# HGRN's score tasks laid at chosen places of the RWKV steps in the scans of a hybrid token mixer

## The chip, the cores and the metric

The kernel runs on one core of a Trainium2 chip. The metric is the device time of one execution in microseconds. The kernel before was timed three times: 5044.99, 5073.87 and 5080.72 us, median 5073.87 us.

## The reference

One layer over 2048 latent tokens and 256 context tokens, all float32: a normed and modulated input is projected, goes through two kinds of scans in both directions, is read out, and a mixture of experts follows. Only the scans matter here.

```python
# HGRN, 4 heads of 128, for each direction, in chunks
bc = cumsum(logf)                                    # within a chunk
o  = (q * exp(bc)) @ s + (causal scores of q, k with decay exp(bc_t - bc_s)) @ v
s  = exp(bc_last) * s + (k * exp(bc_last - bc)).T @ v

# RWKV-7, 8 heads of 64, for each direction, token by token
sa = s @ kk_t
s  = s * w_t - outer(sa, kk_t * a_t) + outer(v_t, k_t)
y_t = s @ r_t
```

The context's final states start the scans of the latent tokens, so each direction of each scan is one chain over 2304 tokens.

## The kernel before, in words

The stages follow one another: modulation, RWKV's projection, HGRN's projection with RWKV's preparation, masks, **scans**, read-out, experts, combination. The diff touches the scans (`scans`, which calls `both_scans` on each engine).

HGRN works in steps of 128 tokens (`HG_STEPS` = 18), RWKV in steps of 64 (`RW_STEPS` = 36), both directions d = 0 and 1 side by side. One turn of `both_scans` is one HGRN step beside two RWKV steps; two turns stand ahead of the loop, and the loop's body holds two.

An RWKV step (`RwkvScan`) does two things. It computes the inverse of a unit triangular matrix of its 64 tokens for every head, by levels: gram products (L1432), a mask on VectorE (L1570), the masks of each level on GpSimd (L1554), a first inverse (L1579), a turn (L1441), and then for the levels 1 to 5 a **cross** product on TensorE (L1453), its copy X on ScalarE (L1514), a **grow** product on TensorE (L1461, L1464) and the **update** of the inverse on VectorE (L1585, at level 5 L1587). Each of these needs the one before it. Beside it runs the chain of the step before: rhs (L1380), solve (L1391), out (L1401), state (L1415), with ScalarE's copies of rhs, u and y (L1492, L1498, L1504) and VectorE's state (L1593). `RW_ORDER` lists the stages of a step; each is done for direction 0 and then for direction 1.

An HGRN step (`HgrnScan`) has 16 tasks t: seven levels and the diagonal, for two directions (t odd is direction 1). At its start ScalarE takes logarithms (L362) and, once VectorE has summed them (L497), a block of exponentials (L370 to L373), with a table load ahead of each; GpSimd multiplies them onto k and q (L399, L401). For each task from 2 on VectorE takes a difference of sums (L474), ScalarE its exponentials (L379, L380), GpSimd the scaled q and k (L411, L412), TensorE the **score** product (L429), VectorE the placing into the scores (L482, L486, L490). Behind scores 3 and 4 TensorE transposes k (L439), which ScalarE copies (L385). At the end come both outputs and states (L450 to L459), copied by ScalarE (L390) and added by VectorE (L509).

What sets the order on each engine is a stream of times. Every generator yields a nominal time ahead of each piece of its work, and `side_by_side` always takes the stream with the smallest time, at build time; on the chip each engine executes its list strictly as written, waiting on semaphores. A turn is 1.0 long; RWKV's steps lie at 0 to 0.5 and 0.5 to 1. The same generators are used for all engines, so each engine's list follows from the same times. The loads (`sync`) are issued by SyncE in a fixed order and aren't part of these streams: RWKV's loads of a step wait until the state of two steps before is done.

```python
def hg_time(t):
    return 0.10 + 0.048 * t
def rw_time(name, d, later=0.0):
    return (2 * RW_ORDER.index(name) + d + 0.5 + later) / (2 * len(RW_ORDER))
```

HGRN's own times: logarithms at 0, sums at 0.02, the block of exponentials at 0.045, score t at `hg_time(t)`, its difference 0.12 before, its exponentials 0.08 before, GpSimd's products 0.04 before, the placing 0.03 after, outputs at 0.90 and 0.95.

Of the kernel before, what the change touches and what calls it, by code (L numbers as in the profile page):

```python
# [92 lines left out]
def peel(eng, count, body):  # L93

    body(0)
    if count > 1:
        with eng.Fori(1, count) as g:
            body(g)
# [201 lines left out]
HG_LOG, HG_SUM, HG_ENDS, HG_OUT = 0.0, 0.02, 0.045, 0.90  # L300


def hg_time(t):

    return 0.10 + 0.048 * t
# [927 lines left out]
def side_by_side(*streams):  # L1233

    live = [[next(x), k, x] for k, x in enumerate(streams)]
    while live:
        first = min(live, key=lambda e: e[0:2])
        first[0] = next(first[2], None)
        if first[0] is None:
            live.remove(first)  # L1240


def shifted(stream, start, scale):

    for time in stream:
        yield start + scale * time
# [62 lines left out]
RW_ORDER = ("gram0 rhs gram1 turn cross1 solve grow1 cross2 out grow2 cross3 grow3 state cross4 grow4 cross5 grow5").split()  # L1309
# [300 lines left out]
                f(d)  # L1610


def both_scans(eng, h, r):

    def turn(g):
        for u in range(2):
            k = 2 * g + u
            two = itertools.chain(shifted(r(eng, 2 * k, 0), 0.0, 0.5), shifted(r(eng, 2 * k + 1, 1), 0.5, 0.5))
            side_by_side(two, shifted(h(eng, k, u), 0.25, 1.0))
    peel(eng, HG_STEPS // 2, turn)  # L1620


def scans(nc, A, S, K):
    with ExitStack() as ctx:
        h, r = HgrnScan(nc, Mem(nc, ctx, "hg"), S, K), RwkvScan(nc, Mem(nc, ctx, "rw"), S, K)
        with nc.Block() as block:
# [10 lines left out]
            @block.gpsimd  # L1637
            def _(pool):
                both_scans(pool, h.pool, r.pool)
                r.store(pool, RW_STEPS)  # L1640
                for d in range(2):
                    pool.wait_ge(r.s[d]["y_stored"], 16 * RW_STEPS)

            @block.scalar
            def _(act):
                both_scans(act, h.act, r.act)
                drain(r.act(act, RW_STEPS, 0, True))
                for d in range(2):
                    act.wait_ge(h.s[f"stored{d}"], 16 * HG_STEPS)

            @block.tensor
            def _(pe):
                both_scans(pe, h.pe, r.pe)
                drain(r.pe(pe, RW_STEPS, 0, True))
# [1085 lines left out]
```

## Time and profile before

| | |
|---|---|
| median of three runs | 5073.87 us (5044.99 to 5080.72) |
| the profiled execution | 5056.55 us, span 5055.0 us |
| TensorE busy | 4322.2 us, 86% of the span |
| VectorE, ScalarE, GpSimd busy | 2222.9, 1249.3 and 1571.8 us |
| mean granted TensorE clock | 0.932 |
| the scans | about 1475 to 3120 us of the span |

A program prints the profile from one execution recorded by the hardware. PE is TensorE, DVE VectorE, ACT ScalarE, POOL GpSimd, PEld TensorE's weight loads. A matmul in float32 leaves two records, so the 16 products of 8 heads and two directions are 32 records. In a timeline row stand the start in us, the length of a merged group of instructions, engine, line, operation, what it writes and reads, the shape and the number of records; in brackets the idle time before it and what ended it. In a row of waits stand who waited, for whom, the us in total, the times and the longest. In a row of stretches each engine has its busy us and its number of instructions; behind them come the granted clock (1.00 is full), the share of DMA and GB/s. "issue" is time for which the profile shows nothing that was waited for.

### The profile page before, as it was taken

The numbers are of one execution on the slowest core, as the hardware profiler recorded it, in microseconds if no ns is written. First come the engines' busy times: TensorE is split into PE (matmuls) and PEld (weight loads), VectorE is DVE, ScalarE is ACT, GpSimd is POOL, SyncE is SP. The second block draws the span as 40 slices with busy tenths as digits, with TensorE's granted clock in tenths as the row PEclk, the third lists the DMA queues.
The fourth block names the chain that finished last, engine by engine and source line by source line (L and its number), as shares of the span: only waits on it lengthen the run. The fifth ranks groups of instructions, "written<-read, shape, count | busy, mean of one in ns | idle before, by whom it ended". The sixth has DMA issues, their size and how long they took to land. (4 is left out here: it accounts for less than half of the span.)

```text
span 5055.0 us, 123964 instructions
## 1 busy us (share of the span) xinstructions
PE 4322.2 (86%) x47554; PEld 2949.2 (58%) x47554; DVE 2222.9 (44%) x4021; ACT 1249.3 (25%) x3133; POOL 1571.8 (31%) x1947
## 2 busy tenths in 40 slices
PE   3999889999968988988888986788599999998980
PEld 1777766666748877877877875444333333333330
DVE  1111157777745454554545544788511111111118
ACT  0000034444423333433323322232000000000002
POOL 0000001101125554554545644444322222221224
PEclk7999989999989999999999998888799999999995
DMA  9411156656532223222232223543576899999866
GB/s 298 153 62 53 59 176 198 201 182 201 200 107 81 71 74 94 74 82 70 74 92 67 75 86 98 158 136 113 187 307 238 351 390 391 389 396 402 347 253 270
DMA packets 321434, 917.00 MB, mean 181 GB/s; under 512 B 72528, under 2 KB 171216, under 8 KB 271600
## 3 DMA queue, kind: packets, MB, share of 16 engines
q1 hardware_dynamic: 266192, 759.98, 42.5%
q0 software_dynamic: 47328, 133.02, 7.3%
q10 hardware_dynamic: 7488, 17.83, 0.9%
q8 instruction: 328, 5.37, 0.5%
q14 instruction: 98, 0.80, 0.1%
HBM read 951.09 MB, written 211.26 MB: 230 GB/s over the span
## 5 line engine op out<-in xcount | busy, mean ns | idle before, releaser
L2468 PE MATMUL exp_gate_up<-exp_w_gate,exp_rows_and_rowsT 128*64 128x512 f32 x1664 | 740.3, 602 | 46.9 <-DMA exp_w_up<-in_moe_w_up_dram 46.0
L2468 PE MATMUL exp_gate_up<-exp_w_up,exp_rows_and_rowsT 128*64 128x512 f32 x1664 | 741.0, 602 | 0.0
L1554 POOL TENSOR_TENSOR rw_A_level<-rw_A_rho_beta,const_level_masks 128x256 f32<-128x256 f32 x432 | 340.3, 804 | 651.2 <-DVE rw_A_rho_beta L1570 394.7
L2468 PEld LDWEIGHTS exp_gate_up<-exp_w_gate,exp_rows_and_rowsT 128*64 128x64 f32 x1664 | 229.0, 139 | 532.7 <-issue 532.5
L721 PE MATMUL rwp_product<-rwp_hT,rwp_w_rw 128*128 128x256 f32 (+1 forms) x2016 | 442.9, 383 | 0.0
L721 PEld LDWEIGHTS rwp_product<-rwp_hT,rwp_w_rw 128*128 128x128 f32 (+1 forms) x2016 | 380.2, 189 | 61.0
L874 PE MATMUL hgp_product<-hgp_hT,const_w_hg 128*128 128x256 f32 x1728 | 393.6, 383 | 15.7 <-DMA hgp_hT<-s_hT 15.7
L2419 DVE TENSOR_TENSOR exp_hidden<-exp_hidden,exp_gate_up 64x512 f32<-64x512 f32 x104 | 71.9, 692 | 744.9 <-ACT exp_hidden L2400 744.9
L2493 PE MATMUL exp_down<-exp_w_down,exp_hiddenT 128*64 128x512 f32 x1664 | 380.0, 598 | 1.4
L874 PEld LDWEIGHTS hgp_product<-hgp_hT,const_w_hg 128*128 128x128 f32 x1728 | 326.5, 192 | 70.3 <-DMA hgp_hT<-s_hT 16.1
L1585 DVE TENSOR_TENSOR rw_inverse<-rw_inverse,rw_inverse_bank 128x512 f32<-128x512 f32 x288 | 196.9, 685 | 347.1 <-PE rw_inverse_bank L1464 345.9
L2400 ACT ACTIVATE exp_hidden<-exp_gate_up 64x512 f32<-64x512 f32 x104 | 61.3, 589 | 968.4 <-PE exp_gate_up L2468 968.4
L2377 POOL DMA_INDIRECT s_yb<-exp_out,exp_row_slot x104 | 104.6, 1006 | 623.5 <-PE exp_rows_turned L2453 496.8
L1461 PE MATMUL rw_inverse_bank<-rw_inverse,rw_X 64*64 64x64 f32 x5760 | 245.1, 226 | 55.1 <-ACT rw_X L1514 42.2
L1453 PE MATMUL rw_inverse_bank<-rw_inverse,rw_A_level 64*64 64x64 f32 x5760 | 231.7, 222 | 45.5 <-DVE rw_inverse L1585 37.4
L411 POOL TENSOR_TENSOR hg_scaled_qk<-hg_qkf,hg_exponent 128x256 f32<-128x256 f32 x252 | 220.5, 875 | 120.0 <-ACT hg_exponent L380 119.7
L871 PE MATMUL hgp_product<-const_w_hg,hgp_hT 128*128 128x512 f32 x576 | 254.0, 596 | 1.9 <-DVEq L859 1.9
L1461 PEld LDWEIGHTS rw_inverse_bank<-rw_inverse,rw_X 64*64 64x64 f32 x5760 | 210.4, 140 | 68.5 <-issue 62.3
L1514 ACT ACTIVATE rw_X<-rw_inverse_bank 128x256 f32<-128x256 f32 x360 | 135.5, 381 | 444.4 <-PE rw_inverse_bank L1453 438.5
L2022 PE MATMUL read_projected<-read_w_out,read_mixT 128*128 128x512 f32 x512 | 236.4, 622 | 4.5 <-DVE read_w_out L1887 2.9
L1453 PEld LDWEIGHTS rw_inverse_bank<-rw_inverse,rw_A_level 64*64 64x64 f32 x5760 | 198.7, 135 | 67.0 <-issue 58.8
L2493 PEld LDWEIGHTS exp_down<-exp_w_down,exp_hiddenT 128*64 128x64 f32 x1664 | 121.3, 136 | 184.8 <-issue 178.8
(392 smaller groups left out, 8094.9 us busy)
## 6 DMA issues: line engine op xcount, KB each, us to landing
exp_w_gate<-in_moe_w_gate_dram SPq DMA_DIRECT2D x208, 1024.0 KB
exp_w_up<-in_moe_w_up_dram SPq DMA_DIRECT2D x208, 1024.0 KB
exp_w_down<-in_moe_w_down_dram SPq DMA_DIRECT2D x104, 2048.0 KB
s_rw_in<-prep_operands SPq DMA_DIRECT2D x72, 514.0 KB, 4.1
rw_operands<-s_rw_in SPq DMA_DIRECT2D x72, 514.0 KB, 5.0
rw_tokens<-s_rw_tm SPq DMA_DIRECT2D x144, 192.0 KB, 5.8
hg_qkf<-s_hg_in SPq DMA_DIRECT2D x36, 768.0 KB, 7.9
mod_w<-in_w_mod_dram SPq DMA_DIRECT2D x24, 1024.0 KB, 26.1
```

What stands on the lines that cost most here:

```text
L411: nc.gpsimd.tensor_tensor(zk, level_views(k, d, l)[1], dk, ALU.mult)
L721: mm = nc.tensor.matmul(mp[o % 2][0:width, 0:GROUP], w_in[:, k, c0 - 5 * D_HG:c0 - 5 * D_HG + width], hT[b][:, k, :], start=(k == 0), stop ...
L871: mm = nc.tensor.matmul(self.mp[o % 4][:], self.hT[b][:, k, j * P:(j + 1) * P], self.w[:, k, c0:c0 + D_HG], start=(k == 0), stop=(k == KD ...
L874: mm = nc.tensor.matmul(self.mp[o % 4][:, 0:GROUP], self.w[:, k, c0:c0 + P], self.hT[b][:, k, :], start=(k == 0), stop=(k == KD - 1))
L1453: i = nc.tensor.matmul(self.pa[d][q, 0, j, :], self.al[d][l % 2][q, j, :], self.rt[u][d][q, 1, j, :], start=True, stop=True)
L1461: i = nc.tensor.matmul(self.pa[d][q, 0, j, :], self.x[d][q, j, :], self.rt[u][d][q, 0, j, :], start=True, stop=True)
L1514: nc.scalar.activation(self.x[d][:], self.pa[d][:, 0], ACT.Copy).then_inc(s["x_ready"], 1)
L1554: nc.gpsimd.tensor_tensor(self.al[d][l % 2][:], self.ar[u][d][:, :, 0, :], self.K["lvc"][:, d, l, :].unsqueeze(1).broadcast_to([P, NPAIR, ...
L1585: V.tensor_tensor(rt[:], rt[:], self.pa[d][:], ALU.add).then_inc(s["r_ready"], 1)
L2022: mm = self.nc.tensor.matmul(self.py[j][:], self.mT[:, k, :], self.w_out[:, k, j * 512:(j + 1) * 512], start=(k == 0), stop=(k == KD - 1))
L2468: i = nc.tensor.matmul(pgu[u][q:q + BLK], xT[:, k, r * BLK:(r + 1) * BLK], w[r][:, k, :], start=(k == 0), stop=(k == KD - 1))
L2493: i = nc.tensor.matmul(pd[u][c * 64 + x:c * 64 + x + BLK], hT[u][:, k, x:x + BLK], wd[r][:, k, c * 512:(c + 1) * 512], start=(k == 0), sto ...
```

## The change

RWKV's times stay. HGRN's times, which were shifted by 0.25, go through an increasing map: score t lands at the place `HG_GAPS[t]`, which is just ahead of a named stage of RWKV (`rw_gap` gives the time at which the stage named begins), and all other work of HGRN is placed between by straight lines. The first six scores lie in the first step of RWKV, the other ten in the second.

```diff
+def rw_gap(step, name):
+    return 0.5 * (step + RW_ORDER.index(name) / len(RW_ORDER))
+HG_GAPS = ([rw_gap(0, x) for x in "cross2 cross3 grow3 grow4 cross5 grow5".split()]
+           + [rw_gap(1, x) for x in "rhs turn cross1 cross2 grow2 cross3 grow3 grow4 cross5 grow5".split()])
+HG_AT = [(0.0, HG_GAPS[0] - 0.10), (0.09, HG_GAPS[0] - 0.01)] + [(hg_time(t), g) for t, g in enumerate(HG_GAPS)] + [(HG_OUT, 1.0), (2.0, 2.1)]
+def in_gaps(stream):
+    for time in stream:
+        k = next(i for i in range(len(HG_AT) - 1) if time < HG_AT[i + 1][0])
+        (t0, g0), (t1, g1) = HG_AT[k], HG_AT[k + 1]
+        yield g0 + (time - t0) * (g1 - g0) / (t1 - t0)
 def both_scans(eng, h, r):
...
-            side_by_side(two, shifted(h(eng, k, u), 0.25, 1.0))
+            side_by_side(two, in_gaps(h(eng, k, u)))
```

Three places show what moves. The number behind a name is a buffer: in `rw_X0` and `rw_X1`, `rw_u0` and `rw_u1` it is the direction.

ScalarE in the second turn, from the copy of X1 at level 2 of the first RWKV step on, before:

```order
L1514 ACTIVATE rw_X1<-rw_inverse_bank1 128x256
L362 ACTIVATE hg_logf1<-hg_qkf11,const_eps 128x512
L1504 ACTIVATE rw_y0<-rw_chain_bank0 128x256
L1504 ACTIVATE rw_y1<-rw_chain_bank1 128x256
L370 ACT_TABLE_LOAD
L370 ACTIVATE hg_decay_from_start0<-hg_logf_sum0 128x512
L372 ACTIVATE hg_decay_to_end0<-hg_logf_sum0 128x128 x4
L373 ACTIVATE hg_decay_chunk0<-hg_logf_sum0 128x4
L370 ACTIVATE hg_decay_from_start1<-hg_logf_sum1 128x512
L372 ACTIVATE hg_decay_to_end1<-hg_logf_sum1 128x128 x4
L373 ACTIVATE hg_decay_chunk1<-hg_logf_sum1 128x4
L1514 ACTIVATE rw_X0<-rw_inverse_bank0 128x256
```

ScalarE in the same turn, from the turned inverse of the first RWKV step on, now:

```order
L1509 ACTIVATE rw_inverse00<-rw_inverse_bank0 128x256
L1509 ACTIVATE rw_inverse01<-rw_inverse_bank1 128x256
L1514 ACTIVATE rw_X0<-rw_inverse_bank0 128x256
L370 ACT_TABLE_LOAD
L370 ACTIVATE hg_decay_from_start0<-hg_logf_sum0 128x512
L372 ACTIVATE hg_decay_to_end0<-hg_logf_sum0 128x128 x4
L373 ACTIVATE hg_decay_chunk0<-hg_logf_sum0 128x4
L1514 ACTIVATE rw_X1<-rw_inverse_bank1 128x256
L370 ACTIVATE hg_decay_from_start1<-hg_logf_sum1 128x512
L372 ACTIVATE hg_decay_to_end1<-hg_logf_sum1 128x128 x4
L373 ACTIVATE hg_decay_chunk1<-hg_logf_sum1 128x4
L1498 ACTIVATE rw_u0<-rw_chain_bank0 128x256
```

The block of HGRN's exponentials (L370 to L373) stood behind the copies of y and ahead of the copies of X at level 3. It now stands in two halves, one on either side of the copy of X1 at level 1, and ahead of the copies of u; the logarithms stand ahead of the turned inverses.

TensorE near the end of the second turn, from the cross product of level 4 in the second RWKV step on, before (L450, further down, is HGRN's output):

```order
L1453 MATMUL rw_inverse_bank0<-rw_inverse10,rw_A_level00 64x64 x8
L1453 MATMUL rw_inverse_bank1<-rw_inverse11,rw_A_level10 64x64 x8
L1461 MATMUL rw_inverse_bank0<-rw_inverse10,rw_X0 64x64 x8
L1464 MATMUL rw_inverse_bank0<-rw_X0,rw_inverse10 64x64 x8
L429 MATMUL hg_score_psum0<-hg_scaled_qk0 64x64 x8
L1461 MATMUL rw_inverse_bank1<-rw_inverse11,rw_X1 64x64 x8
L1464 MATMUL rw_inverse_bank1<-rw_X1,rw_inverse11 64x64 x8
L1453 MATMUL rw_inverse_bank0<-rw_inverse10,rw_A_level01 64x64 x8
L1453 MATMUL rw_inverse_bank1<-rw_inverse11,rw_A_level11 64x64 x8
L429 MATMUL hg_score_psum1<-hg_scaled_qk1 64x64 x8
L1461 MATMUL rw_inverse_bank0<-rw_inverse10,rw_X0 64x64 x8
L1461 MATMUL rw_inverse_bank1<-rw_inverse11,rw_X1 64x64 x8
```

The same place now:

```order
L1453 MATMUL rw_inverse_bank0<-rw_inverse10,rw_A_level00 64x64 x8
L1453 MATMUL rw_inverse_bank1<-rw_inverse11,rw_A_level10 64x64 x8
L429 MATMUL hg_score_psum1<-hg_scaled_qk1 64x64 x8
L1461 MATMUL rw_inverse_bank0<-rw_inverse10,rw_X0 64x64 x8
L1464 MATMUL rw_inverse_bank0<-rw_X0,rw_inverse10 64x64 x8
L1461 MATMUL rw_inverse_bank1<-rw_inverse11,rw_X1 64x64 x8
L1464 MATMUL rw_inverse_bank1<-rw_X1,rw_inverse11 64x64 x8
L429 MATMUL hg_score_psum0<-hg_scaled_qk2 64x64 x4
L1453 MATMUL rw_inverse_bank0<-rw_inverse10,rw_A_level01 64x64 x8
L1453 MATMUL rw_inverse_bank1<-rw_inverse11,rw_A_level11 64x64 x8
L429 MATMUL hg_score_psum1<-hg_scaled_qk3 64x64 x4
L1461 MATMUL rw_inverse_bank0<-rw_inverse10,rw_X0 64x64 x8
```

A score (L429) that stood between the two directions' growth (L1461, L1464) now stands between cross and growth. The next stands between growth and the cross product of level 5, and the last ahead of level 5's growth, where scores used to follow that cross product and that growth. All 16 scores now stand ahead of the last growth.

VectorE in the first step of a turn, from HGRN's prefix sums on, before:

```order
L497 SCALAR_TENSOR_TENSOR hg_logf_sum0<-const_chunk_starts,hg_logf0 128x512
L497 SCALAR_TENSOR_TENSOR hg_logf_sum1<-const_chunk_starts,hg_logf1 128x512
L1585 TENSOR_TENSOR rw_inverse00<-rw_inverse00,rw_inverse_bank0 128x512
L1585 TENSOR_TENSOR rw_inverse01<-rw_inverse01,rw_inverse_bank1 128x512
L474 TENSOR_TENSOR hg_exponent2<-hg_logf_sum0 128x512
L1585 TENSOR_TENSOR rw_inverse00<-rw_inverse00,rw_inverse_bank0 128x512
L1585 TENSOR_TENSOR rw_inverse01<-rw_inverse01,rw_inverse_bank1 128x512
```

The same stages now, from the update of level 1 on:

```order
L1585 TENSOR_TENSOR rw_inverse00<-rw_inverse00,rw_inverse_bank0 128x512
L1585 TENSOR_TENSOR rw_inverse01<-rw_inverse01,rw_inverse_bank1 128x512
L474 TENSOR_TENSOR hg_exponent3<-hg_logf_sum1 128x512
L482 TENSOR_TENSOR hg_scores0<-hg_score_psum0,const_ident64 128x256
L1585 TENSOR_TENSOR rw_inverse00<-rw_inverse00,rw_inverse_bank0 128x512
L474 TENSOR_TENSOR hg_exponent0<-hg_logf_sum0 128x512
L1585 TENSOR_TENSOR rw_inverse01<-rw_inverse01,rw_inverse_bank1 128x512
```

The sums (L497) have gone ahead of the updates of level 1, and an HGRN difference (L474) now stands between the two directions' updates of level 2 (L1585).

## Rows read from the trace of the kernel before

**Rows 1.** Busy time of each engine, granted clock and DMA over the stretch 1520:3100.

```profile
1520.00:3100.00 1580.00, 1401.98 (x33603) 1250.30 (x33601) 796.77 (x1411) 557.06 (x1460) 848.13 (x1050) 0.97 0.26 77
```

**Rows 2.** Who waited for whom on TensorE, 1520:3100: us, times, longest.

```profile
PE rw_inverse_bank L1461 <- ACT rw_X L1514: 40.7, 17, 2.4
PE rw_inverse_bank L1453 <- DVE rw_inverse L1585: 35.8, 90, 1.0
PE rw_inverse_bank L1432 <- DMA rw_tokens<-s_rw_tm: 26.5, 18, 2.3
PE hg_score_psum L429 <- issue: 16.6, 20, 2.5
```

**Rows 3.** TensorE's timeline, first step: start, us, what, [idle before].

```profile
2113.00 0.66 PE L1461 MATMUL rw_inverse_bank<-rw_inverse,rw_X 64*64 64x64 f32 x16
2113.47 0.66 PE L1464 MATMUL rw_inverse_bank<-rw_X,rw_inverse 64*64 64x64 f32 x16
...
2115.10 0.68 PE L1453 MATMUL rw_inverse_bank<-rw_inverse,rw_A_level 64*64 64x64 f32 x16
2115.93 0.68 PE L1453 MATMUL rw_inverse_bank<-rw_inverse,rw_A_level 64*64 64x64 f32 x16 [0.15 <-DVE rw_inverse L1585]
...
2121.52 1.31 PE L1453 MATMUL rw_inverse_bank<-rw_inverse,rw_A_level 64*64 64x64 f32 x32 [0.24 <-DVE rw_inverse L1585]
2125.24 1.12 PE L1461 MATMUL rw_inverse_bank<-rw_inverse,rw_X 64*64 64x64 f32 x16 [2.41 <-ACT rw_X L1514]
2126.12 1.10 PE L1464 MATMUL rw_inverse_bank<-rw_X,rw_inverse 64*64 64x64 f32 x16
```

**Rows 4.** TensorE's timeline, end of first step and second step.

```profile
2136.04 0.69 PE L429 MATMUL hg_score_psum<-hg_scaled_qk 128*64 128x64 f32 x16
2136.65 1.15 PE L1453 MATMUL rw_inverse_bank<-rw_inverse,rw_A_level 64*64 64x64 f32 x32
2137.91 1.15 PE L1461 MATMUL rw_inverse_bank<-rw_inverse,rw_X 64*64 64x64 f32 x32
...
2139.60 0.66 PE L439 MATMUL hg_state_psum<-const_ident,hg_decay_to_end 128*128 128x128 f32 x4
...
2142.64 1.09 PE L1432 MATMUL rw_inverse_bank<-rw_operands 64*64 64x128 f32 x16 [1.36 <-DMA rw_tokens<-s_rw_tm]
...
2155.93 0.63 PE L1453 MATMUL rw_inverse_bank<-rw_inverse,rw_A_level 64*64 64x64 f32 x16
2156.98 0.68 PE L1453 MATMUL rw_inverse_bank<-rw_inverse,rw_A_level 64*64 64x64 f32 x16 [0.42 <-DVE rw_inverse L1585]
...
2175.59 0.63 PE L1453 MATMUL rw_inverse_bank<-rw_inverse,rw_A_level 64*64 64x64 f32 x16
2177.05 0.68 PE L1453 MATMUL rw_inverse_bank<-rw_inverse,rw_A_level 64*64 64x64 f32 x16 [0.82 <-DVE rw_inverse L1585]
```

**Rows 5.** ScalarE's timeline of the same turn.

```profile
2111.83 0.85 ACT L1514 ACTIVATE rw_X<-rw_inverse_bank 128x256 f32<-128x256 f32 x2 [0.40 <-PE rw_inverse_bank L1453]
...
2119.86 1.28 ACT L370 ACT_TABLE_LOAD   x1
2121.15 0.63 ACT L370 ACTIVATE hg_decay_from_start<-hg_logf_sum 128x512 f32<-128x512 f32 x1
...
2124.74 0.63 ACT L1514 ACTIVATE rw_X<-rw_inverse_bank 128x256 f32<-128x256 f32 x2
...
2140.30 0.60 ACT L385 ACTIVATE hg_k_tokens<-hg_state_psum 128x512 f32<-128x512 f32 x1 [1.42 <-PE hg_state_psum L439]
```

**Rows 6.** Busy time and granted clock behind the long wait.

```profile
2128.00:2131.00 3.00, 3.00 (x54) 2.77 (x52) 2.07 (x4) 0.00 (x0) 2.40 (x3) 0.50 0.03 5
```

**Rows 7.** Instructions on the inverse: ns min/median/max, first and last start.

```profile
L1585 DVE TENSOR_TENSOR rw_inverse<-rw_inverse,rw_inverse_bank x288: 661/687/690, 1487.4 to 3094.0; 128x512 f32<-128x512 f32 x144
```

**Rows 8.** HGRN's differences on VectorE: ns min/median/max.

```profile
L474 DVE TENSOR_TENSOR hg_exponent<-hg_logf_sum x252: 677/781/1593, 1498.8 to 3092.5; 128x512 f32<-128x512 f32 x126
```

**Rows 9.** GpSimd's timeline of that turn.

```profile
2123.16 1.26 POOL L399 TENSOR_TENSOR hg_decay_to_end<-hg_qkf,hg_decay_to_end 128x512 f32<-128x512 f32 x1
```

## Prediction

> **What bounds the kernel now.** I began with the stretches of the span. The edit touches only the stage of the two scans, which runs from about 1475 to 3120 us. Over its middle 1580 us TensorE is listed busy for 1402 us at a mean granted clock of 0.97, while VectorE has 797, ScalarE 557 and GpSimd 848 us [rows 1]. The stage is TensorE's, with two kinds of loss on top. One is idle time: 1580 − 1402 = 178 us. The other is reduced clock: 3% of 1580 is 47 us of full-speed time. The stage has 18 turns (one HGRN step beside two RWKV steps), so a turn is about 91 us.
>
> Next, TensorE's waits in that stretch [rows 2]. The longest has one place: 17 waits, 40.7 us, for ScalarE's copy of X. Then 35.8 us in 90 waits of a cross product for VectorE's update of the inverse, and 26.5 us for the operand loads. Waits put down to "issue" (16.6 us before HGRN scores alone) have no releaser and stay.
>
> Then the timeline of one turn. A batch of 16 records of 64x64 starts 0.47 us after the one before it, but is listed as 0.66 us long (2113.00 and 2113.47, [rows 3]). So 0.19 us behind each batch counts as busy though nothing new starts in it: a listed idle time is about 0.19 short of what is really lost. I count from start to start. Direction 1's second-level cross starts 0.83 us after direction 0's (2115.10, 2115.93) where 0.47 would do, and direction 0's starts 0.23 us after the four batches of growth are through (2113.00 + 4 × 0.467 = 2114.87). That is 0.23 + 0.36 = 0.59 us for one uncovered stage. The big wait is at 2125.24: the cross products begun at 2121.52 are through at 2122.45, and growth starts 2.79 us later, because ScalarE had its block of log sums' exponentials ahead of the copy (2119.86 to 2124.74, [rows 5]). Behind this wait the granted clock is 0.50 [rows 6], the lower of its two levels (1.2 GHz of 2.4), and 16 records take 0.88 us instead of 0.47.
>
> **The change part by part.** No instruction is added or removed, and SyncE's queue keeps its order. An HGRN turn used to lie from 0.25 to 1.25 of RWKV's two steps. It now lies from about 0.11 to 1.08, with each score task (16 records, 0.61 us from 2136.04 to 2136.65 [rows 4]) right ahead of an RWKV product that waited. Gains (+) and losses (−) per turn, in us:
>
> 1. First step, cross2: score 0 (0.61) goes ahead of it. The 0.59 above is covered: **+0.59**.
> 2. First step, cross3: lost now 0.24 idle [rows 3] + 0.19 = 0.43. Score 1 goes ahead, but VectorE now has an HGRN difference between the two directions' updates. From the end of direction 0's growth: 0.24 to the update, 0.69 for it [rows 7], 0.78 for the difference [rows 8], 0.69 for the second update, 0.24 back: 2.64. TensorE has 0.93 + 0.61 + 0.47 = 2.01. New loss 0.63: **−0.20**. Second step, the same place: taken as cross2 of that step (item 6), 0.58 is lost now, 0.63 then: **−0.05**.
> 3. ScalarE's block moves from ahead of the third-level copies to between direction 0's and direction 1's first-level copies. The copy at 2111.83 ends at 2112.2; table load 1.29 (2119.86 to 2121.15); one direction's exponentials (2124.74 − 2121.15)/2 = 1.79; copy 0.38: 2115.7, and 0.2 more to release TensorE [rows 5]. Growth of direction 1 would have begun at 2113.93, so it waits 2.0. The second 1.79 delays the copies of u to 2117.9, where TensorE stands at about 2118.4 (it has growth, score 0 and two crosses to do): hidden. Old 2.79, new 2.0: **+0.8**. Bounds: −2.1 (4.9 exposed: 1.29 + 2 × 1.79, rounded) and +2.79.
> 4. Clock. The listed idle time falls from 2.41 to about 1.8, so fewer of these waits should be followed by the lower level. Bounds 0 and 47/18 = 2.6; I take about a quarter: **+0.7**.
> 5. Copy between cross and growth with nothing between: 2136.65 + 0.93 to 2137.91 is 0.33 [rows 4]. Three such places get a score (cross5 of the first step, turn to cross1 and cross4 of the second): **+1.0**.
> 6. Second step, cross2: 2156.98 − 2155.93 − 0.47 = 0.58 [rows 4], because VectorE had two HGRN instructions between the updates; none now, and score 9 ahead: **+0.58**. Cross5: 2177.05 − 2175.59 − 0.47 = 0.99, same cause, gone: **+0.99**.
> 7. Loads. The wait for the second step's operands (2142.64, idle 1.36) averages 26.5/17 = 1.6. SyncE issues them when the first step's state is done; between that and their use TensorE has one transpose more (0.59, from 2139.60 on), minus waits that go: **+0.5**, bounds 0 and 1.6.
> 8. New queueing on ScalarE: the k copy of direction 0 now stands ahead of the fourth-level copy of direction 1, and waits for score 3 and its transposes. From the end of the crosses: 0.61 + 0.59 + 0.2 + 0.60 (2140.30, [rows 5]) + 0.38 + 0.2 = 2.6, where TensorE has 1.20 + 0.93 = 2.13: **−0.45**. Behind that copy stand an exponential and the second k copy; the next to need them, score 6, is over 6 us off.
> 9. New queueing on VectorE: a difference between the two masks of the second step. 0.24 + 0.69 + 0.78 + 0.69 + 0.24 = 2.64 against gram 0.97 + score 0.61 + turn 0.47 = 2.05: **−0.59**.
>
> 10. GpSimd: its four products of k and q (1.26 each [rows 9], 5.0 us in all) now stand ahead of the fourth-level masks and of the scaled operands of score 2. They follow ScalarE's block: over by 2121, masks by about 2122.6, score 2's operands by about 2124.3. TensorE wants them behind cross3, near 2125.6 by my walk: **0**, and −1.2 if all that is 2.4 us later.
>
> Items 1, 5 and 6 are at worst 0 (a score delays what it should cover) and at best as given; items 2, 8 and 9 together lie between 0, if TensorE gets there late anyway, and −4.1 (each difference 1.59 long).
>
> Sum +3.87 us per turn, × 18 = 70 us. The profiled execution took 5056.6 us, so 4987; the median of the runs shown is 17 us above it, and 5073.9 − 70 = 5004.
>
> **A rule to weigh.** The HGRN difference reads two SBUF operands, and its duration runs from 0.68 to 1.59 us round a median of 0.78 [rows 8], while the inverse update, which reads one operand from PSUM, keeps to 0.66 to 0.69 [rows 7]. The Trainium skill, SBUF — State Buffer, section "Who interferes with whom", states that a VectorE instruction with two SBUF inputs contends with a GpSimd instruction that reads SBUF, and that whichever issues second blocks fully. The trace agrees in the spread of the one kind and the evenness of the other. The rule speaks against this change, since three such differences now stand inside the chain of the inverse (items 2 and 9); what full blocking would give is rival B.
>
> **Rivals.**
> A, slower: ScalarE's block is exposed in full. It now stands in the first quarter, where TensorE has no HGRN work to put beside it. If VectorE's prefix sums come late, both halves of the block show. Price: item 3 turns from +0.8 to −2.1, item 4 from +0.7 to −3.0 (about 6 us at 0.50 behind a long wait [rows 6]): 3.87 − 2.9 − 3.7 = −2.7, × 18 = 49 us more, 5123. It decides from a wait of over about 3 us at the first growth. For it: the clock already falls behind 2.41 us. Against it: the walk above hides the second half with 0.5 us to spare.
> B, within 1%: the differences are blocked. Each of the three takes 1.59 instead of 0.78: 3 × 0.81 = 2.4 off, leaving 1.5, × 18 = 27: 5047. For it: the maximum of [rows 8]; against: the median is near the minimum.
> C, much faster: with no wait over 2 us the lower clock all but goes. Item 4 becomes 2.6: 3.87 + 1.9 = 5.8, × 18 = 104: 4970. Against it: waits for "issue" remain.
>
> **How the numbers follow.** Forecast 0.42, B 0.30, C 0.18, A 0.10. A measurement of this kernel tells about 1% (51 us) from no change. Faster by more: 0.85 of the forecast, all of C, a tenth of B: 0.57. Slower: A, 0.09. The rest is 0.34. Range: from below C, with item 7 at its bound (20 us more), 4947, to no gain at all, 5076; A is left out.
>
> **What would show it.** In the new trace the 90 waits for VectorE's inverse update fall from 35.8 us to under 18; the wait for ScalarE's X moves from the third growth to the first and reads about 1.8 us; TensorE's idle time in the stage falls from 178 to 110 to 140 us; the operand loads' wait falls by a third; a turn takes 87 us. The forecast is wrong if the first growth waits over 3 us, or if scores 2 and 3 wait for GpSimd's products.

## The result, and the profile after

The changed kernel took 4992.27 us (4990.99 to 5003.25, four runs) against 5071.93 us before (5044.99 to 5080.72, four runs): a ratio of 0.9854, 95% interval 0.9823 to 0.9885, so faster by more than the 1% that a measurement tells. Three later comparisons of the same pair gave 0.990, 0.985 and 0.988 (table below; the intervals of the first and the last reach 0.993 and 0.991); the four pairs of medians lie 80, 52, 74 and 65 us apart, 68 on average. The forecast was 5004 us, 70 us under.

The profiled execution has a span of 4991.9 us against 5055.0. A memset on VectorE (L515) closes each HGRN step, so its first and last start give the length of a turn: (3111.4 − 1564.2) / 17 = 91.0 us before, and now (3056.3 − 1560.1) / 17 = 88.0. That is the groups view of one line, before and after (ns minimum, median, maximum; first and last start):

```profile
L515 DVE MEMSET const_spare<- x18: 59/59/59, 1564.2 to 3111.4; 128x1 f32 x18
```

```profile
L515 DVE MEMSET const_spare<- x18: 59/59/59, 1560.1 to 3056.3; 128x1 f32 x18
```

The stretch 1520:3060, of before and of after (columns as in [rows 1]):

```profile
1520.00:3060.00 1540.00, 1365.27 (x32630) 1216.60 (x32628) 773.70 (x1371) 544.07 (x1423) 819.92 (x1014) 0.97 0.27 79
```

```profile
1520.00:3060.00 1540.00, 1394.52 (x33791) 1241.46 (x33791) 797.86 (x1414) 550.46 (x1463) 866.40 (x1044) 0.98 0.27 79
```

In the same time TensorE gets through 3.6% more records (33791 to 32630). Its idle time falls from 175 to 145 us.

TensorE's waits in that stretch, after, to be held against [rows 2]:

```profile
PE rw_inverse_bank L1461 <- ACT rw_X L1514: 26.9, 17, 1.7
PE rw_inverse_bank L1461 <- issue: 20.9, 22, 2.2
PE rw_inverse_bank L1432 <- DMA rw_tokens<-s_rw_tm: 16.2, 14, 2.0
PE rw_inverse_bank L1432 <- issue: 13.8, 7, 2.2
PE rw_inverse_bank L1453 <- issue: 12.1, 9, 1.8
PE rw_chain_bank L1405 <- issue: 8.9, 9, 1.4
PE rw_inverse_bank L1464 <- issue: 8.9, 8, 1.4
PE rw_inverse_bank L1453 <- DVE rw_inverse L1585: 7.9, 14, 0.6
```

Of the 87 waits for VectorE's update in this stretch 14 are left, 34 us down to 8; ScalarE's X costs 27 instead of 41; the loads 16 instead of 26. Added up over all rows of the view, waits for another engine or a DMA fall from 114 to 66 us, but "issue" rises from 52 to 77. So 25 of the 49 us that the waits gave came back as idle time with no releaser.

The first step of one turn on TensorE (start, length, what, [idle before]), which answers to [rows 3]:

```profile
1653.15 1.13 PE L1391 MATMUL rw_chain_bank<-rw_rhs,rw_inverse 64*64 64x64 f32 x32
1654.09 0.66 PE L1461 MATMUL rw_inverse_bank<-rw_inverse,rw_X 64*64 64x64 f32 x16
1654.55 0.66 PE L1464 MATMUL rw_inverse_bank<-rw_X,rw_inverse 64*64 64x64 f32 x16
1656.92 0.68 PE L1461 MATMUL rw_inverse_bank<-rw_inverse,rw_X 64*64 64x64 f32 x16 [1.71 <-ACT rw_X L1514]
1657.41 0.66 PE L1464 MATMUL rw_inverse_bank<-rw_X,rw_inverse 64*64 64x64 f32 x16
1658.00 1.04 PE L429 MATMUL hg_score_psum<-hg_qkf 128*64 128x64 f32 x16
1658.96 1.97 PE L1453 MATMUL rw_inverse_bank<-rw_inverse,rw_A_level 64*64 64x64 f32 x32
```

The long wait has moved to the first growth, and score 0 stands behind that growth. The cross product at 1658.96 lists 1.97 us for 32 records, where 1.15 is usual: the trace's clock records have the lower level (1.2 of 2.4 GHz) for 3.4 us from 1658.1, behind the wait.

ScalarE in the same turn, answering to [rows 5]:

```profile
1652.92 0.38 ACT L1514 ACTIVATE rw_X<-rw_inverse_bank 128x256 f32<-128x256 f32 x1 [0.52 <-PE rw_inverse_bank L1453]
1653.32 1.28 ACT L370 ACT_TABLE_LOAD   x1
1654.61 0.63 ACT L370 ACTIVATE hg_decay_from_start<-hg_logf_sum 128x512 f32<-128x512 f32 x1
1655.15 1.26 ACT L372 ACTIVATE hg_decay_to_end<-hg_logf_sum 128x128 f32<-128x128 f32 x4
1656.32 0.19 ACT L373 ACTIVATE hg_decay_chunk<-hg_logf_sum 128x4 f32<-128x4 f32 x1
1656.41 0.36 ACT L1514 ACTIVATE rw_X<-rw_inverse_bank 128x256 f32<-128x256 f32 x1
```

From 1653.32 to 1656.41 direction 1's copy stands behind the table load and one direction's exponentials. Growth should have begun at 1655.03 (1654.09 + 2 × 0.467) and began at 1656.92: 1.9 us, where the prediction walked to 2.0.

### The profile page after: what moved, and what is told of

Same layout as the page of the kernel before. It is cut to its first block and busy times, and to the rows that moved or that the text cites. A ratio compares the mean times of both kernels' runs of the same rounds, so it can differ in the third digit from the quotient of the medians.

```text
span 4991.9 us, 123964 instructions
## 1 busy us (share of the span) xinstructions
PE 4301.2 (86%) x47554; PEld 2933.0 (59%) x47554; DVE 2225.5 (45%) x4021; ACT 1240.0 (25%) x3133; POOL 1594.4 (32%) x1947
## 5 line engine op out<-in xcount | busy, mean ns | idle before, releaser
L1554 POOL TENSOR_TENSOR rw_A_level<-rw_A_rho_beta,const_level_masks 128x256 f32<-128x256 f32 x432 | 366.6, 867 | 549.6 <-DVE rw_A_rho_beta L1570 415.6
L874 PEld LDWEIGHTS hgp_product<-hgp_hT,const_w_hg 128*128 128x128 f32 x1728 | 326.6, 192 | 70.5 <-DMA hgp_hT<-s_hT 16.2
L1585 DVE TENSOR_TENSOR rw_inverse<-rw_inverse,rw_inverse_bank 128x512 f32<-128x512 f32 x288 | 197.2, 685 | 313.6 <-PE rw_inverse_bank L1464 312.4
L1461 PE MATMUL rw_inverse_bank<-rw_inverse,rw_X 64*64 64x64 f32 x5760 | 242.8, 223 | 50.9 <-ACT rw_X L1514 29.2
L1461 PEld LDWEIGHTS rw_inverse_bank<-rw_inverse,rw_X 64*64 64x64 f32 x5760 | 203.9, 136 | 68.8 <-issue 59.8
L1453 PE MATMUL rw_inverse_bank<-rw_inverse,rw_A_level 64*64 64x64 f32 x5760 | 219.7, 223 | 25.2 <-issue 12.1
L411 POOL TENSOR_TENSOR hg_scaled_qk<-hg_qkf,hg_exponent 128x256 f32<-128x256 f32 x252 | 195.6, 776 | 122.8 <-PE hg_score_psum L429 65.7
L2486 PEld LDWEIGHTS exp_gate_up<-exp_w_up,exp_rows_and_rowsT 128*64 128x64 f32 x1664 | 229.5, 139 | 0.0
```

The costliest lines, as they stand in the source:

```text
L411: nc.gpsimd.tensor_tensor(zk, level_views(k, d, l)[1], dk, ALU.mult)
L874: mm = nc.tensor.matmul(self.mp[o % 4][:, 0:GROUP], self.w[:, k, c0:c0 + P], self.hT[b][:, k, :], start=(k == 0), stop=(k == KD - 1))
L1453: i = nc.tensor.matmul(self.pa[d][q, 0, j, :], self.al[d][l % 2][q, j, :], self.rt[u][d][q, 1, j, :], start=True, stop=True)
L1461: i = nc.tensor.matmul(self.pa[d][q, 0, j, :], self.x[d][q, j, :], self.rt[u][d][q, 0, j, :], start=True, stop=True)
L1554: nc.gpsimd.tensor_tensor(self.al[d][l % 2][:], self.ar[u][d][:, :, 0, :], self.K["lvc"][:, d, l, :].unsqueeze(1).broadcast_to([P, NPAIR, ...
L1585: V.tensor_tensor(rt[:], rt[:], self.pa[d][:], ALU.add).then_inc(s["r_ready"], 1)
```

## The experiments

All in one table. A ratio is to runs of the kernel before on the same chip; a turn is the distance of L515's starts over 17; lower clock is the sum of the trace's clock records at 1.2 GHz that begin between 1480 and 3000 us and before the scans end. The kernel before took 5057.15 us beside `again`, `even`, `between` and `block_late`, 5073.19 beside `again2`, `block_split`, `diffs_out` and `padded`, and 5067.14 beside `again3`, `diffs_4`, `split_and_diffs` and `all`. Medians are of four to six runs, of ten for `even` and of two for `padded`.

| run | median us | ratio, 95% interval | span | turn | lower clock, us |
|---|---|---|---|---|---|
| before | 5071.93 | | 5055.0 | 91.0 | 85 |
| change | 4992.27 | 0.9854 [0.9823, 0.9885] | 4991.9 | 88.0 | 75 |
| again | 5005.04 | 0.9900 [0.9873, 0.9928] | 4987.8 | 87.5 | 41 |
| again2 | 4999.03 | 0.9849 [0.9807, 0.9891] | 5021.9 | 89.2 | 120 |
| again3 | 5002.17 | 0.9879 [0.9845, 0.9912] | 4983.2 | 87.2 | 44 |
| even | 5019.51 | 0.9927 [0.9905, 0.9948] | 5017.1 | 89.2 | 75 |
| between | 5017.65 | 0.9922 [0.9897, 0.9947] | 5007.4 | 88.6 | 51 |
| block_late | 4988.1 | 0.9871 [0.9839, 0.9902] | 4985.0 | 86.9 | 38 |
| block_split | 4947.29 | 0.9763 [0.9724, 0.9803] | 4938.8 | 84.8 | 27 |
| diffs_4 | 4982.6 | 0.9842 [0.9809, 0.9875] | 4978.7 | 86.9 | 48 |
| diffs_out | 4952.3 | 0.9776 [0.9733, 0.9820] | 4949.6 | 85.1 | 31 |
| split_and_diffs | 4941.23 | 0.9748 [0.9721, 0.9774] | 4939.5 | 84.2 | 17 |
| all | 4930.38 | 0.9739 [0.9709, 0.9769] | 4919.0 | 83.5 | 24 |
| padded | 5151.31 | 1.0160 [1.0093, 1.0226] | 5168.0 | 97.4 | 154 |

**The change again, and its places taken away.** `again` is the changed kernel unaltered. `even` keeps the first score's place and the earlier window, and spaces the scores evenly; `between` moves every score half a stage later:

```diff
+HG_GAPS = [HG_GAPS[0] + 0.051 * t for t in range(HG_TASKS)]
```

```diff
+HG_GAPS = [g + 0.5 / 34 for g in HG_GAPS]
```

> The changed kernel once more, beside the others. Both theories: 0.985 of before, within its interval of 0.982 to 0.989.

> HGRN's 16 scores stand at equal distances over the same part of the turn instead of ahead of chosen stages; everything before score 0 and behind score 15 keeps its place. Theory of the places (the gain is that a score stands exactly where a product would wait): about half of items 1, 5 and 6 of the prediction (3.2 us per turn) is lost again, 1.5 us per turn or 27 us: ratio 0.990 to 0.993. Rival, theory of the window (the gain is that HGRN's work lies inside the two RWKV steps, ahead of the last growth, wherever it is): 0.985.

> Every score is moved on by half a stage, so that it stands between the two directions' products of the stage it stood ahead of. Theory of the places: copy gaps (cross to growth) stay covered, since direction 0's copy has the score beside it; update gaps (growth to cross) lose the 0.23 us ahead of direction 0's cross again and get VectorE's scores placing between the updates, 0.3 us at some 7 places and more where a difference falls in between: 2 us per turn, ratio 0.991 to 0.995. Rival, theory of the window: 0.985.

Against `again`, which ran beside them, they lose 14 and 13 us (20 and 18 against 4999.6 us, the mean of the change's four medians) of the 68: 70 to 75% of the gain stay when the chosen places are gone. Both ratios lie in the ranges that the theory of the places gave (0.990 to 0.993, 0.991 to 0.995), and the 0.985 of the theory of the window alone is outside both intervals. But `again` itself came out at 0.990, and its interval overlaps theirs; what tells the kernels apart is all 16 runs of the change (mean 5001 us) against 5025 and 5018. So the places are worth about a quarter, and what is left, which these runs do not divide further, goes with the earlier window and what it does to ScalarE's and VectorE's lists. In `between` the waits are as long in sum (147 us against 143) but elsewhere; its largest row is ScalarE's block once more, now ahead of the copy of the turned inverse:

```profile
PE rw_inverse_bank L1453 <- ACT rw_inverse L1509: 36.3, 17, 2.1
```

**ScalarE's block behind the copies of u.**

```diff
-            yield HG_ENDS + 0.015 * d
+            yield 0.0885 + 0.001 * d
```

> ScalarE's block of exponentials is moved behind the copies of X1 at level 1 and of u, otherwise as changed. Theory (item 3 of the prediction): the first growth's wait of 1.7 us is gone, the block lies beside two outputs (2.8 us) and more, and the lower clock behind that wait with it: 1.6 to 2.2 us per turn, 29 to 40 us, ratio 0.977 to 0.980. Rival: the block comes late for GpSimd, and score 2 waits for its operands instead: 0.984 to 0.987, with a wait of 1 us or more at a score.

4988.1 us: 0.9871, in the spread of the change itself (0.985 to 0.990) and not the 0.977 to 0.980 of the theory. The rival's reading holds. The wait for X at the first growth is gone, and another as long has taken its place, for GpSimd, whose products need the block:

```profile
PE hg_score_psum L429 <- POOL hg_scaled_qk L412: 25.4, 16, 1.6
```

The block cannot be moved as a whole: early it stops TensorE through the copy of X, late through GpSimd's operands.

**The block in halves.** Each direction's exponentials behind those of task 2 or 3, and GpSimd's products likewise (the lines of what follows shift by up to 4).

```diff
-        for d in range(2):
-            yield HG_ENDS + 0.015 * d
+        def ends(d):
...
+            if t in (2, 3):
+                yield (0.144, 0.208)[t - 2]
+                ends(t - 2)
```

> ScalarE's block in two halves, each behind an exponential of the tasks: direction 0 behind that of task 2 and the copies of y, direction 1 behind that of task 3 and the copies of X at level 3; GpSimd's products of k and q behind the scaled operands of tasks 2 and 3. Theory (the first growth and score 2 waited for the one chain block, products, operands, and each half fits beside TensorE's other work): both the wait for ScalarE's X (26.9 us in all) and the wait of scores for GpSimd (25.4 us with the block late) are under 5 us; 1.6 us per turn and a part of the lower clock, 27 to 40 us under the change. Rival (TensorE is bound by the supply of its instructions, idle time called issue takes the place): issue rises by 10 us or more and the gain is under 15 us.

4947.29 us, 52 us under the 4999.6 of the change. That is more than the 27 to 40 us expected, and "issue" did not rise (71 us against 77), so its rival fell. Of the waits for ScalarE's block and for the products behind it only this is left, though not under the 5 us expected, and the loss at the first growth, from start to start, falls from 2.03 to 0.11 us:

```profile
PE hg_score_psum L433 <- POOL hg_scaled_qk L413: 11.2, 16, 0.8
```

The places add up to this gain only with one that nobody had forecast. Per turn the first growth gives 1.92 us and the score behind the fourth growth loses 0.82 (0.34 to 1.16). Cross3 of step 1 gives 0.59, because with GpSimd's products moved away the difference between VectorE's updates there takes 0.68 us in 17 of 18 turns (1.28 in the change, see below). Together that is 1.69 × 18 = 30 us, and 48 us less of lower clock in the profile is worth another 24.

**The differences out of the pairs on VectorE.** All three, and only the first:

```diff
-        order = sorted([(hg_time(t) - 0.12, 0, t) for t in range(2, HG_TASKS)] + [(hg_time(t) + 0.03, 1, t) for t in range(HG_TASKS)])
+        order = sorted([(hg_time(t) - 0.12 + (0.004 if t in (4, 10, 14) else 0.0), 0, t) for t in range(2, HG_TASKS)] + [(hg_time(t) + 0.03, 1, t) for t in range(HG_TASKS)])
```

In `diffs_4` the condition is `t == 4`.

> The differences of tasks 4, 10 and 14 are moved from between VectorE's two updates (or masks) to behind them. Items 2 and 9 of the prediction: cross3 of the first step no longer waits for the update (0.6 to 0.9 us lost per turn), nor cross3 and turn of the second (0.4 and 0.35): 1.2 us per turn, 22 us under the change. Rival (these waits lie beside others or beside the supply of instructions): under 8 us.

> Of the three differences of the recurrence that the changed kernel puts between the inverse's two updates on VectorE, only the one of task 4 (between the updates of crossings 3 of step 1) goes behind them; 10 and 14 (between the two masks of step 2) stay. Moving all three was measured at 0.977 of the time before against 0.985 to 0.990 for the change. If the updates' pair in step 1 carries it (the step named in the prediction, 0.43 to 0.63 us lost there), this kernel should get 15 to 25 us of the 40 to 47: 4975 to 4990 us, with the wait for the update on VectorE at crossings 3 of step 1 down from a loss of 0.96 us to some 0.4. If the two masks carry it, the time stays at that of the change within 8 us. The third reading is that most of it is the clock: all three moved left 31 us of lower clock against 75; then the time follows the lower clock of its own profile, 0.5 us for each us of it.

4952.3 and 4982.6 us. The second alone does not stand clear of the change: its interval overlaps that of `again3` beside it. What it does is seen in the trace. VectorE's timeline at the second update of step 1, in the changed kernel, with the GpSimd instruction that is at work when the difference starts:

```profile
2280.87 0.69 DVE L1585 TENSOR_TENSOR rw_inverse<-rw_inverse,rw_inverse_bank 128x512 f32<-128x512 f32 x1 [3.65 <-PE rw_inverse_bank L1464]
2281.47 1.29 DVE L474 TENSOR_TENSOR hg_exponent<-hg_logf_sum 128x512 f32<-128x512 f32 x1
2282.69 0.68 DVE L1585 TENSOR_TENSOR rw_inverse<-rw_inverse,rw_inverse_bank 128x512 f32<-128x512 f32 x1
```

```profile
2281.38 0.83 POOL L412 TENSOR_TENSOR hg_scaled_qk<-hg_qkf,hg_exponent 128x256 f32<-128x256 f32 x1
```

In an earlier turn, with GpSimd idle:

```profile
1665.14 0.69 DVE L1585 TENSOR_TENSOR rw_inverse<-rw_inverse,rw_inverse_bank 128x512 f32<-128x512 f32 x1 [5.17 <-PE rw_inverse_bank L1464]
1665.75 0.68 DVE L474 TENSOR_TENSOR hg_exponent<-hg_logf_sum 128x512 f32<-128x512 f32 x1
1666.35 0.68 DVE L1585 TENSOR_TENSOR rw_inverse<-rw_inverse,rw_inverse_bank 128x512 f32<-128x512 f32 x1
```

and with the differences out:

```profile
1660.89 0.69 DVE L1585 TENSOR_TENSOR rw_inverse<-rw_inverse,rw_inverse_bank 128x512 f32<-128x512 f32 x1 [5.17 <-PE rw_inverse_bank L1464]
1661.73 0.69 DVE L1585 TENSOR_TENSOR rw_inverse<-rw_inverse,rw_inverse_bank 128x512 f32<-128x512 f32 x1 [0.15 <-PE rw_inverse_bank L1464]
1662.34 0.68 DVE L474 TENSOR_TENSOR hg_exponent<-hg_logf_sum 128x512 f32<-128x512 f32 x1
```

The second update starts 1.82 us after the first in the first of these, 1.21 in the second, 0.84 with the difference out. The first case is the usual one: this difference takes over 1 us in 14 of 18 turns (median 1.28), and 0.68 in three. TensorE loses 0.81 us at direction 1's cross in the median turn, 0.23 in the three, and 0.05 with the difference out; so the difference costs 0.18 by standing there and 0.6 more by being held up beside GpSimd. Counted up to the score behind it, the loss at cross3 of step 1 falls from 0.96 us to 0.15 in both runs: 0.81 × 18 = 15 us (12 by the mean), and `diffs_4` is 17 us under the change. The other two differences, which are hardly held up (medians 0.73 and 0.68 us), give 0.35 − 0.15 at the turn and 0.37 − 0.15 at cross3 of step 2, 8 us together. The remaining 24 us or so of `diffs_out` are not in the waits that were removed: the "issue" gap at the last cross of step 2 (below) went from 8 times 1.49 to 2 times 0.88, 10 us, and its profile has 44 us less of lower clock than the change's, worth half of that. How much of this a typical execution has, one profile doesn't tell.

**"Issue".** Where these gaps lie can be counted in matmul records from the start of the loop's body (two turns, 3856 records in every pass). Over eight bodies of the change, gaps of 0.3 us and more sit at exactly the same records: 15 (behind the branch back, 7 times, 1.97 us on average), 1196 (7, 1.40), 1814 (8, 1.49), 3163 (8, 0.77), 3287 (8, 1.08) and 3534 (8, 1.11). Before, most are there too, but shorter or rarer (15: 7 of 1.92; 1197: 7 of 0.65; 1815: 5 of 1.26; 3288: 8 of 0.73; 3536: 2 of 0.37), with others that the change doesn't have (2799: 4 of 1.07). The same counts hold where other stages stand at them: `even` has 15, 1195, 1814 and 3534. The one at 1814 opens in the middle of a cross product's 32 records, where the list has no wait at all. `padded` tests whether the gaps belong to the stream of TensorE's own instructions: it repeats a semaphore increment, which nobody waits for, twice more ahead of each RWKV stage, 136 instructions per turn.

```diff
             pe.sem_inc(self.turns, 1)
+            pe.sem_inc(self.turns, 1)
+            pe.sem_inc(self.turns, 1)
```

> Two more semaphore instructions without a wait ahead of each RWKV stage on TensorE: 272 more instructions in the two turns of the loop's body, nothing else. If the idle time called issue is the supply of instructions, which runs out at a fixed count of instructions, its places move to earlier records in the body (the one at record 1800 to about 1740, the one at 3560 to about 3430). Rival (it belongs to the products that stand there): the same records. The time itself rises by what 136 instructions per turn cost, 1 to 3 us per turn.

5151.31 us, far more than either theory said. The turn grows by 9.3 us over the change's 88.0, 69 ns for each added instruction. "Issue" doubles from 77 to 151 us. Of its places neither reading had all: none is left at 1196 or 1814, and none came at 1740; the largest are at 919 (2.19 us on average), 1869 (2.09) and 2822 (2.01), but 3175, 3295 and 3535 (0.84 to 0.92) are where gaps were. Its two largest rows of that kind:

```profile
PE rw_inverse_bank L1477 <- issue: 32.9, 41, 3.0
PE rw_inverse_bank L1442 <- issue: 28.2, 21, 2.8
```

So the idle time follows the number and place of TensorE's own instructions, not another engine. Part of the rise is the added instructions themselves: gaps with a semaphore instruction in them or just ahead grew from 14 to 60 us, the others from 63 to 91. What makes the gaps, the supply of instructions or something else in TensorE's sequence, is not shown.

**Both together, and k's copy later.** `split_and_diffs` joins the two edits. `all` has one more:

```diff
-                yield hg_time(t - 2) + 0.025
+                yield hg_time(t - 2) + 0.025 + (0.004 if t == 5 else 0.0)
```

> The changed kernel once more, beside the next three runs. Its three profiles so far had spans of 4991.9, 4987.8 and 5021.9 us with 75, 41 and 120 us of lower clock in the scans (1480 to 3000 us), so the clock alone moves one execution by up to 40 us. Expected: 4990 to 5015 us, and lower clock between 40 and 120 us.

> The block of exponentials in two halves (4947 us alone) and the three differences behind the paired work (4952 us alone) in one kernel. If the waits stand one behind another in TensorE's row, they add up: 45 to 50 us and 40 to 47 us under the change, some 4905 to 4920 us, 83 us per turn, with under 10 us of waits for ScalarE and under 10 for VectorE in 1520 to 3060 us. If both gained chiefly through the clock (27 and 31 us of lower clock left of 75), the second brings only its waits, 8 to 14 us and a few us of clock: 4930 to 4940 us. What stays in either is the idle time at fixed places of the loop's body, 60 to 80 us.

> As the run before, and the copy of k for the fifth task starts 0.004 of a turn later on ScalarE, behind the copy that the fourth growth of step 1 waits for. The prediction priced that queueing at 0.45 us per turn (8 us); the trace of the changed kernel shows 0.32 lost there in place of 0.08. Expected by that: 3 to 6 us under the run before, a gain below what five rounds separate; the loss at that growth goes back to 0.1 us. The rival: the copy of k is then late for GpSimd's gated product and for the turn of k, and costs as much as it gives.

4941.23 and 4930.38 us. The two gains of 52 and 47 us don't add up; the second reading, 4930 to 4940, is the nearer. Over the block in halves alone (4947.29 us) the differences then bring 6 us, which is not clear of noise (0.9748 and 0.9763, with overlapping intervals). The joined kernel waits longer for GpSimd:

```profile
PE hg_score_psum L433 <- POOL hg_scaled_qk L413: 20.5, 16, 1.4
```

The wait stands at score 4, behind the fourth growth of step 1, and the loss from that growth to the score goes from 1.15 us (block in halves) to 1.76. Counted from the start of cross3, TensorE is ready 0.23 us earlier than with the block in halves (9.57 against 9.80), and the score starts 0.39 us later (11.34 against 10.95). The second part has a cause in the trace: the difference of task 4, moved behind the updates, now starts just ahead of GpSimd's product L402 of direction 0, which takes 1.72 us instead of 1.27. The 0.61 us per turn are more than the 0.44 that the differences gave at cross3 (0.37 to 0.15 in each of the two steps). A new "issue" gap has come as well, 8 times 1.06 us at record 2918. `all` has the same 1.76 us there, because the wait for GpSimd covers k's copy; its 11 us under `split_and_diffs` are within the intervals (0.9739 and 0.9748 overlap nearly whole). That the loss there would go back to 0.1 us was wrong.

## Why the prediction was right

The median of this comparison is 12 us under the forecast, and the four comparisons' mean of 68 us is 2 off its 70. Part of that is errors that cancel. By the steps, with the loss at a place counted start to start and the median over the turns (before to after, us; gains +):

- Item 1, cross2 of step 1, +0.59: 0.22 + 0.39 to 0.01 + 0.05, **+0.55**. Right.
- Item 2, cross3 of step 1, −0.20: 0.44 ahead of it to 0.10 ahead and 0.81 at direction 1, **−0.47**; of step 2, −0.05: 0.73 to 0.37, **+0.36**. The first is over twice its price, the second has the other sign, and the sum is −0.11 for −0.25. `diffs_4` confirms the mechanism, VectorE's difference between the updates of step 1. But that 0.81 lies near the walk's 0.63 is luck. The walk added the listed lengths, 0.69 + 0.78 + 0.69, where VectorE's instructions start 0.60 us apart (1665.14, 1665.75, 1666.35): unhindered, the loss is 0.23, not 0.63. The 0.6 us that bring it to 0.81 are the difference held up beside GpSimd, which the walk left to rival B.
- Item 3, ScalarE's block, 2.79 to 2.0: 2.79 to 2.05 at the first growth, and 0.14 stays between cross3 and the score that now follows it, **+0.60** for +0.8. Right. `block_late` shows that it could not be had by moving the block as a whole, `block_split` that nearly all of it could in halves.
- Item 4, lower clock, +0.7: 99 us of it in 1520:3060 before, 68 after; half of the difference over 17 turns is **+0.9**. Right in this pair, though see below; the four profiles of the change spread by more than the whole term.
- Item 5, three copy gaps, +1.0: cross5 of step 1 0.33 to 0.18, cross4 of step 2 0.33 to 0.13, and turn of step 2 0.42 to 0.35, **+0.42** (item 9 is in the last of them). Too high: a score covers the copy, but 0.13 to 0.18 stays.
- Item 6, cross2 of step 2 +0.58: 0.73 to 0.05, **+0.68**. Cross5 +0.99: 1.14 to 0.14 in every second turn, **+1.00**, but 1.5 to 2.4 in the others, where the "issue" gap at record 1814 falls into that very place; by the mean 1.55 to 1.03, +0.52.
- Item 7, loads, +0.5: 1.86 to 1.38, **+0.48**. Right in this pair; the waits for the loads, 25.6 us before, are 16.2 here, but 17.1, 19.6 and 23.7 in the other three profiles of the change.
- Item 8, k's copy, −0.45: 0.08 to 0.32, **−0.24**. Right sign, half the size.
- Item 9, a difference between the masks, −0.59: taking it out gave 0.20. Too high, by the same listed lengths as item 2, and here nothing held the difference up; it is counted with item 5.
- Item 10, GpSimd, 0: no wait for its products in the change at all. Right; with the block later they decide, by 0.7 to 1.6 us a turn.

The items' gains come to +4.3 per turn, away from "issue" (0.55 − 0.47 + 0.36 + 0.60 + 0.9 + 0.42 + 0.68 + 1.00 + 0.48 − 0.24), where 3.87 was forecast. The step that failed is a sentence of the first part: waits put down to "issue" "have no releaser and stay". They grew by 25 us in 17 turns, −1.5 per turn, part of it right in the place that item 6 had cleared. 4.3 − 1.5 = 2.8, and the turn fell by 3.0. So the scans gave 51 us between the first and the last turn's end and 4 more in the first turn, and the other 8 of the profile's 63 lie behind the scans, in stages that the change doesn't touch (1943.6 us behind the last L515 before, 1935.6 after, but 1941 in `again` and `again3` and 1945 in `again2`). That the gaps grow because TensorE waits less for others is argued only: it holds between before and after, but `even`, with waits for others of 75 us against 66, has 60 of "issue" against 77.

Of "what would show it", the waits for the update (under 18: 8), the move to the first growth (about 1.8: 1.7), the loads (a third: 37% less here, 7 to 33% in the other three profiles) and the turn (87: 88.0, 87.5, 89.2, 87.2) came as said; idle time did not reach 110 to 140 us (145), for that reason.

Three slips of arithmetic in the prediction change nothing: C with item 7 at its bound is 4970 − 20 = 4950 and not 4947, no gain at all is 5074 and not 5076, and items 2, 8 and 9 at three differences of 1.59 come to −3.7 and not −4.1. The "about 6 us at 0.50" of rival A is not in [rows 6], whose window is 3 us; the stretches behind this wait in the change were 3.4 us.

**The rivals.** A fell: the second half of the block was hidden, and the wait stayed at 1.7 us. C fell: 41 to 120 us of lower clock remain, though with block and differences out of the way it comes into reach (17 us in `split_and_diffs`, 24 in `all`). B came true at one of its three places: the difference of task 4 was held up, to 1.28 us and not 1.59, and those of tasks 10 and 14 hardly at all (medians 0.73 and 0.68). It cost 8 us in all (0.68 by the mean instead of 0.23, × 18) where B had 43. Its mechanism is in the trace to the hundredth. What a difference loses is what the GpSimd instruction under which it starts still has to do:

```profile
1658.71 0.93 DVE L474 TENSOR_TENSOR hg_exponent<-hg_logf_sum 128x512 f32<-128x512 f32 x1
```

```profile
1657.82 1.27 POOL L401 TENSOR_TENSOR hg_decay_from_start<-hg_qkf,hg_decay_from_start 128x512 f32<-128x512 f32 x1
1659.06 1.71 POOL L399 TENSOR_TENSOR hg_decay_to_end<-hg_qkf,hg_decay_to_end 128x512 f32<-128x512 f32 x1
...
1664.12 0.84 POOL L412 TENSOR_TENSOR hg_scaled_qk<-hg_qkf,hg_exponent 128x256 f32<-128x256 f32 x1
1667.26 0.73 POOL L1554 TENSOR_TENSOR rw_A_level<-rw_A_rho_beta,const_level_masks 128x256 f32<-128x256 f32 x1 [2.29 <-PE rw_inverse_bank L1453]
```

At 1658.71 the product of 1657.82 had 0.38 us to go, and the difference took 0.25 more than the 0.68 that it takes alone (1665.75, in the idle time ahead of the last row). At 2281.47 (above) the product had 0.74 to go, and it took 0.61 more. In the changed kernel 160 differences start with over 0.15 us of a GpSimd product or mask to go, and in all of them the excess is that rest less 0.14 us, within 0.01. The other 92 took 0.67 to 0.69 us. Then the GpSimd instruction that starts under the difference is the longer one: the product of 1659.06 took 1.71 us, one with nothing beside it 1.27. The Trainium skill's rule (SBUF — State Buffer, "Who interferes with whom") calls the shared ports an exclusive lock and says of VectorE's two-port modes that whoever issues second blocks fully. The trace shows the same for this instruction with two SBUF operands, in both directions. Between 1480 and 3000 us the median difference took 0.93 us (0.81 before) and the longest 1.33, so the 1.59 of the rival did not occur in this trace; it is the usual length of task 4's difference in `split_and_diffs`.

## What to carry to other kernels

- In a chain of dependent stages over three engines, what stands between the two directions' copies or updates on ScalarE and VectorE costs more than where the filler stands on TensorE: moving the scores off their places cost 13 to 20 us, moving one block and three differences out of the pairs gave 58, though the clock has a share in that.
- Two edits that each shorten the same chain don't add up: look for the engine that is next in line (here GpSimd, 0.7 to 1.5 us a turn), and run them joined before summing.
- Price an instruction on VectorE by the distance of starts, not by its listed length, and look up what GpSimd has at work when it starts: the same difference took 0.68 or 1.29 us by that alone.
- Don't carry idle time without a releaser over as a constant. Count at which record it falls, and price a stage that will stand there by it.

## What the runs showed of the hardware

**Short idle time can be followed by long stretches at the lower clock.** Behind [rows 6] stood 2.41 us of idle time; here 1.56 us, put down to "issue", stood ahead, and the lower level then stayed for 20.5 us, through all of HGRN's outputs (TensorE of the changed kernel, then the stretch's busy times and clock):

```profile
2066.13 0.50 PE L1453 MATMUL rw_inverse_bank<-rw_inverse,rw_A_level 64*64 64x64 f32 x9 [1.56 <-issue]
2066.56 0.68 PE L429 MATMUL hg_score_psum<-hg_scaled_qk 128*64 128x64 f32 x8
2067.16 1.53 PE L1461 MATMUL rw_inverse_bank<-rw_inverse,rw_X 64*64 64x64 f32 x32
2068.63 0.79 PE L450 MATMUL hg_out_psum<-hg_state,hg_decay_from_start 128*128 128x128 f32 x2
```

```profile
2068.00:2088.00 20.00, 20.00 (x94) 12.65 (x90) 1.95 (x6) 1.19 (x2) 0.00 (x0) 0.50 0.41 133
```

The same wait of 1.71 us at the first growth occurs in 15 turns and was followed by the lower level in only 3 of them. So the clock is the noisiest part of this stage: four profiles of one program have 75, 41, 120 and 44 us of it, with spans from 4983.2 to 5021.9 us. A term such as item 4 can be forecast as a tendency only, and two profiles should not be compared more closely than some 40 us.

**A TensorE instruction without any work is not free here.** Each added semaphore increment lengthened the turn by 69 ns (9.3 us / 136). About half of the 9.3 shows as "issue" (4.4 us per turn to 9.5), and some 2.8 is more time at the lower clock (4.3 us per turn to 9.8, at half speed).

**VectorE and GpSimd hold each other up whole.** HGRN's difference, which reads two SBUF operands, took longer by the rest of the GpSimd instruction at work, less 0.14 us, in 160 of 160 cases, and in the other order GpSimd's was the longer (1.71 for 1.27 us). The order of two starts decides which engine pays, and so moving a VectorE instruction out of one chain can put its 0.4 us into GpSimd's, as in `split_and_diffs`.
